# A fifth two-level weight product in the FFN loop of a retention/S5 block, in a new order of pairs

## What is computed

```python
h = rmsnorm(x, norm_ffn_g)
x = x + (silu(h @ w_gate) * (h @ w_up)) @ w_down
return rmsnorm(x, norm_final_g)
```

## Time and profile before

| what | value |
|---|---|
| median of 3 runs | 1094.08 us |
| lowest and highest run | 1093.38 and 1094.35 us |
| the profiled execution, its own time | 1094.19 us |
| its span on the core | 1092.1 us |
| granted clock of TensorE, mean | 0.998 |
| bytes read from HBM | 218.09 MB |

### The profile page before, as it was taken

One profiled execution on the slowest core, in us unless ns is written; L12 is line 12 of the kernel. 1 busy time (PEld: TensorE's weight loads), 2 busy tenths in 40 slices (PEclk: granted clock), 3 DMA queues, 4 the chain that ended last, 5 costly groups with the idle time before them and its releaser, 6 DMA issues.

```text
span 1092.1 us, 15574 instructions
## 1 busy us (share of the span) xinstructions
PE 1080.7 (99%) x5386; PEld 892.1 (82%) x5386; DVE 936.1 (86%) x1043; ACT 601.1 (55%) x738; POOL 189.9 (17%) x322
## 2 busy tenths in 40 slices
PE   9999999999999999999999999999999999999997
PEld 7878778888988888888888888888888888888886
DVE  7999998754875788989898998989899898989987
ACT  7569544445753565545555464655546465555544
POOL 7130143320100320311030302003030300303011
PEclk9999999999999999999999999999999999999999
DMA  9884588864665677666576666658566665757662
GB/s 360 286 232 147 179 235 242 268 191 150 212 218 187 205 221 229 214 206 212 197 230 220 185 228 204 201 191 241 200 210 214 207 206 182 229 192 231 214 213 113
DMA packets 123802, 232.18 MB, mean 213 GB/s; under 512 B 12016, under 2 KB 19568, under 8 KB 123120
## 3 DMA queue, kind: packets, MB, share of 16 engines
q1 hardware_dynamic: 113392, 215.10, 61.1%
q0 software_dynamic: 9952, 15.62, 5.4%
q10 hardware_dynamic: 416, 0.92, 0.2%
HBM read 218.09 MB, written 5.11 MB: 204 GB/s over the span
## 4 chain that ended last, share of the span: by engine, by line
PE 80%; DVE 13%; DMA 3%; issue 2%; ACT 1%; DVEq 0%; POOL 0%; SPq 0%; POOLq 0%; ACTq 0%
PE ps L1787 36%; PE ps L1751 31%; DVE w_lo L941 4%; PE ps L1778 3%; PE ps L1771 3%; PE ps L1775 3%; DMA raw<-in_w_in 2%; DVE w_lo L947 1%; DVE wb L1074 1%; DVE wb L1072 1%; ACT w_hi L544 1%; DVE wb_t L1073 1%; PE ps L2095 1%; PE ps L2096 1%; PE ps L2097 1%
## 5 line engine op out<-in xcount | busy, mean ns | idle before, releaser
L550 ACT ACTIVATE w_hi<-raw 128x1024 fp32r<-128x1024 f32 (+1 forms) x166 | 156.7, 955 | 191.2 <-PE ps L1787 117.7
L544 ACT ACTIVATE w_hi<-raw 128x1024 fp32r<-128x1024 f32 x135 | 142.7, 1060 | 154.0 <-DMA raw<-in_w_in 53.2
L941 DVE TENSOR_TENSOR w_lo<-raw,w_hi 128x1024 fp32r<-128x1024 f32 x136 | 163.8, 1220 | 63.7 <-ACT w_hi L544 63.1
L424 POOL DMA_DIRECT2D ff_moved<-ff_turned x184 | 97.0, 536 | 601.7 <-DVE ff_turned L1365 543.3
L947 DVE TENSOR_TENSOR w_lo<-raw,w_hi 128x1024 fp32r<-128x1024 f32 (+1 forms) x166 | 176.3, 1088 | 23.7 <-ACT w_hi L550 22.9
L550 ACT ACTIVATE w_hi<-raw_more 128x1024 fp32r<-128x1024 f32 x82 | 84.5, 1054 | 54.9 <-PE ps L1751 36.5
L947 DVE TENSOR_TENSOR w_lo<-raw_more,w_hi 128x1024 fp32r<-128x1024 f32 x82 | 97.4, 1218 | 8.4 <-ACT w_hi L550 8.4
L559 ACT ACTIVATE mix_hi<-mix 128x1024 fp32r<-128x1024 f32 x80 | 83.5, 1056 | 21.9 <-DVE mix L1312 15.2
L1323 DVE TENSOR_TENSOR mix_lo<-mix,mix_hi 128x2048 fp32r<-128x2048 f32 x40 | 91.4, 2285 | 0.0
L1751 PE MATMUL ps<-w_hi,ffT_hi 128*128 128x512 f32 x320 | 85.6, 389 | 0.0
L1751 PE MATMUL ps<-w_lo,ffT_hi 128*128 128x512 f32 x320 | 85.6, 389 | 0.0
(11 more groups left out here) (362 smaller groups left out, 2238.4 us busy)
## 6 DMA issues: line engine op xcount, KB each, us to landing
raw<-in_w_in SPq DMA_DIRECT2D x79, 512.0 KB, 5.4
raw<-in_w_gate SPq DMA_DIRECT2D x68, 512.0 KB, 3.9
raw<-in_w_up SPq DMA_DIRECT2D x68, 512.0 KB, 4.6
raw<-in_w_down SPq DMA_DIRECT2D x46, 512.0 KB, 4.1
raw_more<-in_w_down SPq DMA_DIRECT2D x42, 512.0 KB, 4.5
raw<-in_w_out SPq DMA_DIRECT2D x32, 512.0 KB, 4.1
raw_more<-in_w_gate SPq DMA_DIRECT2D x20, 512.0 KB, 4.5
raw_more<-in_w_up SPq DMA_DIRECT2D x20, 512.0 KB, 5.5
```

Of the source, the lines that this page charges most:

```text
L424: eng.dma_start(moved[32 * b:32 * b + 32, :, a].rearrange("p t k j -> p t (k j)"), turned[32 * a:32 * a + 32, b].rearrange("p t k j -> p t ...
L544: nc.scalar.activation(w_hi[:, n % SPL], raw[:, n % RAW], ACT.Copy).then_inc(S["high_done"], 1)
L550: nc.scalar.activation(w_hi[:, c % SPL, at], raw_of(c)[:, at], ACT.Copy).then_inc(S["high_done"], 1)
L941: tt(w_lo[:, n % SPL], raw[:, n % RAW], w_hi[:, n % SPL].bitcast(F32), ALU.subtract).then_inc(S["low_done"], 1)
```

## The change

Pair 2 becomes a mixed pair, pair 4 becomes plain and pair 5 becomes mixed; pairs 0, 1, 3, 6 and 7 stay. So there are five mixed pairs for four, and the order goes from C S C S S C S C to C S S S C S S C. The fifth pair's token sums get a place of their own (`sD_hi`, `sD_lo`), `combos` can now make the sums of two mixed pairs at once, and the choice among the two buffers of the mixed weights counts within the turn, since five is odd.

```diff
-UNITS = "CSCSSCSC"
+UNITS = "CSSSCSSC"
...
-             ("sC_hi", [P, 4, 2, P], F32R), ("sC_lo", [P, 4, 2, P], F32R)],
+             ("sC_hi", [P, 3, 2, P], F32R), ("sC_lo", [P, 3, 2, P], F32R), ("sD_hi", [P, 4, P], F32R), ("sD_lo", [P, 4, P], F32R)],
...
-            [("mix_hi", [P, 2, 4, NCOL], F32R), ("mix", [P, 4, NCOL], F32), ("s_sum", [P, 6, P], F32)],
+            [("mix_hi", [P, 2, 4, NCOL], F32R), ("mix", [P, 4, NCOL], F32), ("s_sum", [P, 8, P], F32)],
...
                     if turn is not None and step == 1:
-                        act.wait_ge(S["mix_free"], count(turn, NM, q))
-                    nc.scalar.activation(mix_hi[:, q % 2, half_], mix[:, half_], ACT.Copy).then_inc(S["mix_high"], 1)
+                        act.wait_ge(S["mix_free"], count(turn, NM, q + (NM % 2 and q == NM)))
+                    nc.scalar.activation(mix_hi[:, q % NM % 2, half_], mix[:, half_], ACT.Copy).then_inc(S["mix_high"], 1)
...
-                _, _, one = column_combos(c)
                 pair = h_sum[:].rearrange("p (u k) (t s) -> p u k t s", u=2, t=TOK)
...
+                mixed = []
+                for i, (sums, _) in enumerate(combo_parts(c)):
+                    if 2 * c + i in MIXED:
+                        a11, a21, a12, a22 = (pair[:, i, k, t] for k in range(2) for t in range(TOK))
+                        tt(sums[:, 0], a21, a22, ALU.add).then_inc(S["h_summed"], 1)
+                        tt(sums[:, 2], a21, a11, ALU.subtract)
+                        mixed.append((sums, a11, a12))
+                    else:
+                        last = tt(sums, pair[:, i, :, 0], pair[:, i, :, 1], ALU.subtract)
...
-                tt(mix_lo[:, q % 2], mix[:], mix_hi[:, q % 2].bitcast(F32), ALU.subtract).then_inc(S["mix_low"], 1)
+                tt(mix_lo[:, q % NM % 2], mix[:], mix_hi[:, q % NM % 2].bitcast(F32), ALU.subtract).then_inc(S["mix_low"], 1)
```

More of the change, by code:

```diff
@@ L224, in build @@
             [("below_h2B_hi_room", [P, VEC_COLS], F32), ("h2B_hi", [P, 8, SEQ], F32R), ("h2B_lo", [P, 8, SEQ], F32R),
-             ("sC_hi", [P, 4, 2, P], F32R), ("sC_lo", [P, 4, 2, P], F32R)],
+             ("sC_hi", [P, 3, 2, P], F32R), ("sC_lo", [P, 3, 2, P], F32R), ("sD_hi", [P, 4, P], F32R), ("sD_lo", [P, 4, P], F32R)],
         )
-        s_plain = [[m["sC_hi"][:, i] for i in range(4)], [m["sC_lo"][:, i] for i in range(4)]]
+        s_last = m["sD_hi"], m["sD_lo"]
+        s_plain = [[m[name][:, i] for i in range(len(PLAIN))] for name in ("sC_hi", "sC_lo")]
         y1A_hi, y1A_lo, y1B_hi, y1B_lo, cl, k_tab, decays, wb_t, x_in, h2B_hi, h2B_lo = (
@@ L254, in build @@
             s_mixed[part] += [x[:, i] for i in range(2)]
+        for part in range(2):
+            s_mixed[part].append(s_last[part][:])
         wbT, dec, sT = (m[k] for k in ("wbT", "dec", "sT"))
@@ L363, in mixed_pair, with combo_parts @@
             return c % TURN < 2 * GRP and c % TURN // 2 in MIXED
-        def column_combos(c):
-            one = 2 * c if 2 * c in MIXED else 2 * c + 1
-            return MIXED.index(one), PLAIN.index(4 * c + 1 - one), one - 2 * c
+        def combo_parts(c):
+            first, parts = 0, []
+            for u in (2 * c, 2 * c + 1):
+                width = 4 if u in MIXED else 2
+                to = [s_mixed[part][MIXED.index(u)] if u in MIXED else s_plain[part][PLAIN.index(u)] for part in range(2)]
+                parts.append((s_sum[:, first:first + width], to))
+                first += width
+            return parts
         def act_block(kb, part):
@@ L572, in combo_high @@
                 act.wait_ge(S["s_summed"], c + 1)
-                i, k, _ = column_combos(c)
-                nc.scalar.activation(s_mixed[0][i], s_sum[:, 0:4], ACT.Copy).then_inc(S["s_hi"], 1)
-                nc.scalar.activation(s_plain[0][k], s_sum[:, 4:6], ACT.Copy).then_inc(S["s_hi"], 1)
+                for sums, (hi, _) in combo_parts(c):
+                    nc.scalar.activation(hi, sums, ACT.Copy).then_inc(S["s_hi"], 1)
             def xh(r):
@@ L1277, in combos @@
             def combos(c):
-                _, _, one = column_combos(c)
                 pair = h_sum[:].rearrange("p (u k) (t s) -> p u k t s", u=2, t=TOK)
-                (a11, a21), (a12, a22) = ([pair[:, one, k, t] for t in range(TOK)] for k in range(2))
-                plain = pair[:, 1 - one]
-                dve.wait_ge(S["h_summed"], 3 * c + 1)
+                done = sum(1 + 2 * (u in MIXED) for u in range(2 * c)) - c
+                dve.wait_ge(S["h_summed"], done + 1)
                 if c:
@@ L1294, in combo_low @@
+                for i, (sums, a11, _) in enumerate(mixed):
+                    dve.wait_ge(S["h_summed"], done + 2 + i)
+                    tt(sums[:, 1], sums[:, 0], a11, ALU.subtract).then_inc(S["h_summed"], 1)
+                for i, (sums, _, a12) in enumerate(mixed):
+                    dve.wait_ge(S["h_summed"], done + 2 + len(mixed) + i)
+                    last = tt(sums[:, 3], a12, sums[:, 1], ALU.subtract)
+                last.then_inc(S["s_summed"], 1)
             def combo_low(c):
-                i, k, _ = column_combos(c)
@@ L1297, in combo_low @@
                 dve.wait_ge(S["s_hi"], 2 * c + 2)
-                tt(s_mixed[1][i], s_sum[:, 0:4], s_mixed[0][i].bitcast(F32), ALU.subtract).then_inc(S["s_lo"], 1)
-                tt(s_plain[1][k], s_sum[:, 4:6], s_plain[0][k].bitcast(F32), ALU.subtract).then_inc(S["s_lo"], 1)
+                for sums, (hi, lo) in combo_parts(c):
+                    tt(lo, sums, hi.bitcast(F32), ALU.subtract).then_inc(S["s_lo"], 1)
             def mix_sums(c, turn=None):
```

## The result

| | before | with the change |
|---|---|---|
| median, same chip | 1093.73 us (1093.16 to 1094.35) | 1115.38 us (1114.87 to 1117.16) |
| profiled execution, its span | 1094.19, 1092.1 us | 1117.16, 1115.2 us |
| a turn | 62.83 us | 64.76 us |

The ratio is 1.0201, 95% interval 1.0183 to 1.0218: 2.0% slower, 1.4 us above the forecast of 1114.0 and inside its range.

A forecast was written before the change was run, and what follows sets the result against it. PE's matmuls bound the kernel before; with the change PE waits for DVE. 2.8 us for the first turn plus 9 x 1.9 make 19.9 on 1094.19, so 1114.1, taken as 1114.0 against the median; range 1109 to 1119.

The forecast's parts named there:

- The run on DVE: In the loop, DVE walked operation by operation from 681.61 to pair 6; PE waits for it, a turn 1.9 us longer.
- The marks it named: Loop signs: L1336's successor every 64.7 us, PE waits at pairs 2, 3, 6, longest 1.5 to 1.8 ahead of pair 3.
- What a wait costs beyond DVE's end: Where PE waits for DVE in the loop: PE starts 0.05 us later, its first two matmuls take another 0.12.
- Start to start, not the durations in full: DVE steps overlap in the loop; the rival, chance 0.05, lost 0.08 at each of 12 steps: 0.96 a turn, 1123.6 us.
- The first turn: Loop's first turn, walked from DVE reaching pair 2 at 441.20: first `w_down` chunk 2.8 us later.
- a cover: Ahead of the loop: three more `combos` operations, 1 us at most, hidden by DVE's 3.40 us idle time, costing nothing.
- the work fits: Rival, chance 0.06: DVE's added work fits its idle time, PE never waits, a turn loses 0.68 us: 1087.3 us.
- only the turn's end is late: Rival, chance 0.06: DVE in time for the pairs, only first sums at turn's end late; ten turns 8.4 us more, 1102.5.
- the clock falls: Rival, chance 0.02: PE's pauses drop its clock; twelve matmuls a turn at 1.2 GHz add 2.72 us: 1141 us.
- the cost of a meeting point: Where PE and DVE arrive together in the loop, the wait costs 0.05 to 0.4 us, so 1.5 to 2.4 a turn.

## Why the prediction was right, and where it wasn't

**The run on DVE: right.** It was walked from 681.61; the same low part stands at 693.08 in the turn shown above, 11.47 later. Shifted by that, the forecast and the trace are:

| | forecast | trace |
|---|---|---|
| PE starts pair 2 | 707.59 | 707.60 |
| pair 2's mixed weights | 709.80 | 709.80 |
| PE starts pair 3 | 714.24 | 714.25 |
| PE starts pair 6 | 729.69 | 729.71 |
| PE starts pair 7 | 734.77 | 734.79 |
| first chunk of `w_down` | 740.27 | 740.23 |

A turn is longer by 64.76 - 62.83 = 1.93 us, where 1.9 was taken from 1.85 to 1.96. Nine turns are 17.4 us. The marks it named are there: L1350 every 64.76 us (64.7); waits at pairs 2, 3 and 6; the idle time at the seventh pair's low parts gone; the longest wait ahead of pair 3. That wait reads 1.42 in brackets, where 1.6 was forecast from start to start: the idle time counts from the recorded end of the last matmul, which is 0.39 long, while its successor could have started 0.23 after it. DVE's idle time ahead of the last sums is 1.68, just outside the 1 to 1.6 that were named.

**What a wait costs beyond DVE's end: right.** 0.05 was taken from the earlier trace rows and 0.12 for slow first matmuls; it is 0.05 to 0.07, two first matmuls are recorded 0.09 to 0.12 longer than elsewhere, and three take 0.96 to 0.98 in place of 0.84.

**Start to start, not the durations in full: right.** `mix_low` starts at 707.46 while the two low parts from 705.73 end at 707.55. Durations in full would have lost 0.96 us a turn, by the prediction's estimate of 12 steps of 0.08. The Trainium skill, "VectorE: DVE Perf Modes", The DRAIN you can't avoid, says that the next operation doesn't start until the pipeline is empty, and adds that one that isn't held starts earlier. The trace agrees with the addition, which the prediction didn't take in: `mix_low` starts 0.09 us ahead of the recorded end.

**The first turn: the walk right, a cover wrong.** L1350 first starts at 481.6, L1336 at 475.7: 5.9 us later, where 2.8 were forecast. The step that failed is "Ahead of the loop `combos` has three more operations ... nothing". DVE ahead of the loop with the change, from the token sums of pairs 2 and 3 to pair 1's sums:

```profile
406.69 0.28 DVE L1296 TENSOR_TENSOR s_sum<-h_sum 128x128 f32<-128x128 f32 x1
...
421.05 1.23 DVE L949 TENSOR_TENSOR w_lo<-raw,w_hi 128x1024 fp32r<-128x1024 f32 x1 [3.40 <-ACT w_hi L553]
...
430.79 2.35 DVE L955 TENSOR_TENSOR w_lo<-raw,w_hi 128x1024 fp32r<-128x1024 f32 x2
...
435.18 1.23 DVE L1326 TENSOR_TENSOR mix<-raw 128x1024 f32<-128x1024 f32 x1 [2.04 <-DMA raw<-in_w_up]
```

and in the second trace of the kernel before:

```profile
405.72 0.28 DVE L1286 TENSOR_TENSOR s_sum<-h_sum 128x128 f32<-128x128 f32 x1
...
429.01 2.35 DVE L947 TENSOR_TENSOR w_lo<-raw,w_hi 128x1024 fp32r<-128x1024 f32 x2
...
432.67 1.23 DVE L1312 TENSOR_TENSOR mix<-raw 128x1024 f32<-128x1024 f32 x1 [1.31 <-DMA raw<-in_w_up]
```

From these token sums to the low parts of pair 0 it is 429.01 - 405.72 = 23.29 us here, 23.27 in the first trace of before (405.56 to 428.83), and 430.79 - 406.69 = 24.10 with the change; the eight other traces with five mixed pairs have 24.10 to 24.12. So the combos cost 0.82 us. How the sums are spread over the pairs counts in this too: the run with four mixed pairs in the new order has as many sums in this stretch as the kernel before, and 429.17 - 406.15 = 23.02 us. The idle time of 3.40 us that was named as their cover was none: it is still 3.40 us long, at 421.05 where it was at 419.10. DVE waits there for ACT, and ACT had waited for DVE's sums before. ACT ahead of the gap, before and with the change:

```profile
414.60 0.63 ACT L574 ACTIVATE sB_hi<-s_sum 128x512 fp32r<-128x512 f32 x1 [1.17 <-DVE s_sum L1292]
```

```profile
416.55 0.42 ACT L583 ACTIVATE sC_hi<-s_sum 128x256 fp32r<-128x256 f32 x1 [2.13 <-DVE s_sum L1306]
...
419.96 2.95 ACT L553 ACTIVATE w_hi<-raw 128x1024 fp32r<-128x1024 f32 x3
```

ACT gets the sums 1.95 us later, and the gap ends 1.95 us later: 1.13 that the stretch had begun later, and the 0.82. So the delay is passed on through ACT and comes out whole behind the gap. An idle time covers work only if what ends it doesn't hang on that work.

The rest of the 5.9 splits in three. The token sums of pairs 2 and 3 began 1.13 us later (406.69 against 405.56), behind work that is the same in both but for the order of pair 0's and pair 1's sums; over the traces of this study they begin between 404.64 and 408.32, so I take this for scatter. The wait for pair 1's load was 1.10 us longer (2.04 against 0.94), and that scatters too: 1.31 in the second trace of before, 0.95 to 2.32 with five mixed pairs. Its least is 0.95 where it was 0.94 before, so nothing shows that it took up any of the 0.82. From pair 1's sums to L1350, the stretch that the prediction walked, it is 481.6 - 435.18 = 46.4 us, against 43.6 and 43.5 in the two traces of before: 2.8 to 2.9, as forecast. The stretch behind the loop is the same: 1092.1 - 1041.2 = 50.9 and 1115.2 - 1064.4 = 50.8 us. In sum 17.4 + 2.8 + 0.8 = 21.0 us by the change; the medians differ by 21.65, the two spans by 23.1 with 2.2 of scatter in it.

**The rivals.** That the work fits fell too: DVE is busy for 61.31 of 65 us, so it fits in sum, and it costs 2% all the same. That only the turn's end is late fell with PE's wait ahead of pair 3. That the clock falls is wrong for the loop, with one exception. In the first turn PE waits for 2.47 us ahead of pair 2, and then:

```profile
448.68 0.73 PE L1801 MATMUL ps<-w_hi,actA_hi 128*128 128x512 f32 x2 [2.47 <-DVE w_lo L955]
```

```profile
449.00:450.00 1.00, 1.00 (x5) 0.76 (x4) 1.00 (x1) 0.45 (x1) 1.00 (x3) 0.71 0.82 88
450.00:451.00 1.00, 1.00 (x4) 0.81 (x3) 0.97 (x2) 0.00 (x0) 1.00 (x2) 0.50 0.91 287
451.00:452.00 1.00, 1.00 (x3) 0.79 (x3) 1.00 (x1) 0.00 (x0) 1.00 (x3) 0.50 1.05 402
452.00:453.00 1.00, 1.00 (x4) 0.77 (x3) 0.93 (x3) 0.80 (x1) 1.00 (x3) 0.58 1.06 404
453.00:454.00 1.00, 1.00 (x6) 0.83 (x5) 1.00 (x2) 0.69 (x2) 0.14 (x1) 1.00 0.66 185
```

From 449 to 453 the granted clock is down at 0.50, 1.2 GHz, for some 3.4 us by the four means. It costs nothing here, since PE would have waited for pair 3's `w_lo` anyway: that is done at 455.27, and PE starts at 455.33. With the plain pair at 3 the clock falls at the same place, and the slack seems to come out of a later wait: ahead of pair 6 PE waits 0.27 us in the first turn and 1.36 in a middle one. So the sign that the prediction named for this rival, a clock below 1.00 in the loop, was met in the first turn alone. No experiment took the clock's fall away, so what it would cost in a turn with no wait behind it stays open.

**Chances and range.** The forecast had 0.80, its range of 10 us came from the cost of a meeting point, and the result lies 1.4 above the middle. Of that 0.8 is the cover that was none, and 0.3 is nine turns at 1.93 for 1.9. The 0.4 us at the upper end of that cost stood in no row, and no trace shows it: the dearest point in the changed kernel's turn is 0.07 us and some 0.12 of slower first matmuls. So the range was wider than the rows asked for.

## What to carry to other kernels

When work moves from the bounding engine to one that is 86% busy, walk the second engine's queue from the last point where it was held up to each point where the first needs it: the same 512 columns cost 0.60 us a turn in that run and nothing some 9 us later, and a mere change of order cost 2.1%. An idle stretch covers added work only where its end is set by something that doesn't depend on that work; the combos' 0.8 us went through a gap of 3.40 us unharmed. And when work is taken off the late engine, look first at what it will wait for next: of 2 us taken out here, 0.49 went to a wait for PE and 0.52 to one for ACT, and 0.8 were won.

## What the hardware showed that was not expected

- A POOL operation on 1024 columns took 3.21 us, and DVE's on 512 columns took 2.75 us beside it in place of 0.69, while the 1024-column one ahead of it, also beside it in part, kept its 1.22.
- A pause of 2.47 us on PE was followed by a stretch at 1.2 GHz, one of 1.42 us in each later turn never was. In the other traces of the study the pause at that place was 2.46 to 2.52 us with a fall behind it (four kernels), and 2.04 to 2.49 us without one (five kernels); since 2.49 had none and 2.46 had one, its length alone doesn't decide at this size. What does was not tried.
- The last stretch ahead of the loop starts up to 3.7 us apart from run to run (404.64 to 408.32 at the token sums of pairs 2 and 3), while a turn repeats to 0.01 us: 62.83 and 62.84 before, 64.76, 64.76 and 64.77 with five mixed pairs. Where a change acts in a loop, the turn tells what the median of three or four runs can't.
